# Up-projections with 512-column matmuls and a later add; modulation sums 20 to 23 on GpSimd

## The chip, the cores and the metric

The kernel runs on one core of a Trainium2 chip. The metric is the device time of one execution in microseconds (us), the median of several runs. Engines are TensorE (PE; PEld is its weight load), VectorE (DVE), ScalarE (ACT), GpSimd (POOL) and SyncE (SP), which here only issues the DMAs of the weights.

## The reference

Two transformer layers on 256 tokens with width 2048, in float32. The part that matters here is the end of the first layer:

```python
sh1, sc1, g1, sh2, sc2, g2 = split(silu(c) @ w_ada + b_ada, 6)      # w_ada: 2048 x 12288
h2 = modulate(rms_norm(x_new, norm2_w), sh2, sc2)                    # 256 x 2048
u = h2 @ w_up                                                        # w_up: 2048 x 11264
u = sum(pad(u)[:, j:j + T] * conv_w[j] for j in range(3)) + conv_b   # along the tokens
gate, val = split(u, 2)                                              # 5632 columns each
x_new = x_new + g2 * ((silu(gate) * val) @ w_down)                   # w_down: 5632 x 2048
```

`g2` is the last sixth of the modulation vector: parts 20 to 23 of it in the kernel, 512 numbers each.

## The kernel before

**Weights as a stream.** All weights pass through TensorE once, as one stream of chunks of 512 KB (`Stream`), in an order that is written out: two row blocks of 128 rows (k) by 512 columns. SP walks the stream (L519): for each chunk it waits until the chunk that last had the same place in SBUF is released, then issues the DMA. The waits are in program order, so one place that is late holds back every later chunk. A place is the least recently used one. There are four places, and up to job `uv1` three more; from then on each chunk takes the place of the chunk four before it in the stream.

**High and low parts.** To keep float32 accuracy on the fast matmul path, ACT rounds a chunk into a high part (`round_chunk`, L1324) and DVE subtracts to get the low part (`rest_chunk`, L1921); that subtraction releases the place. There are three pairs of such parts, so the rounding of chunk s waits for the matmuls of chunk s-3. ACT and DVE both work two chunks ahead of PE in program order. Products are hi\*act_hi, hi\*act_lo and lo\*act_hi (`three`), accumulated in PSUM by `gemm_chunk` (L648).

**Up-projections.** `w_up` has 22 jobs of 8 chunks, `ug0`, `uv0`, ..., `ug10`, `uv10` (gate and value, four tiles of 128 features each). Six pairs (96 chunks) run, then the first part of the down-projection (`downa`), then five pairs (80 chunks) and `downb`. A chunk is 2 k x 4 tiles x 3 products = 24 matmuls of 256 columns (all tokens). Two tiles share a PSUM bank: gate jobs use banks 0 and 1, value jobs 2 and 3. Sixteen steps of `hidden_units` run beside a pair: ACT scales the middle tap out of PSUM (`centre`, L1689), DVE adds the outer taps (`taps`, L2350, L2352), then the gate (L2370, L2373) and the split into `fR` (L1939, L1941).

**Modulation parts 20 to 23.** Each has eight chunks of `w_ada`, which stand in the stream beside the first six pairs: `beside(..., 5, 2, 14)` puts two of them among every five chunks of `w_up`, alternately after three and after two. With two DVE instructions of 512 columns per chunk, `sum_chunk` multiplies each of the chunk's two row blocks by a number per partition and adds it to `rows[a % 2]` (L1970, L1973), in DVE's program order right after a `rest_chunk`. That releases the chunk's place (semaphore `modulation_summed`). After the eighth, PE adds over the partitions into bank 5 (`ada_fold`, L745) and DVE adds the result to `g2b` (`spread_keep`, L1991). POOL issues a few DMAs in this part of the kernel and computes nothing.

Of the kernel before, what the change touches and what calls it, by code (L numbers as in the profile page):

```python
# [11 lines left out]
ACT = mybir.ActivationFunctionType  # L12
# [48 lines left out]
def shape_constants():  # L61
# [11 lines left out]
    def rotation(half):  # L73
# [48 lines left out]
       ("qn0", 2112, 384), ("qn1", 2496, 384), ("ks", 3200, 192), ("kvw", 3392, 460)]  # L122
O2_PAIRS = [6, 7, 4, 5, 0, 1, 2, 3]
# [16 lines left out]
for _names in (["gq", "gr0", "gr1", "dq0", "dq1"] + [f"{k}{n}" for k, c in (("gate", 8), ("pg", 4), ("pd", 4), ("out", 4))  # L140
                                                      for n in range(c)],
               [f"u{'gv'[v]}{i}" for i in range(KF // 4) for v in range(2)],
               [f"downa{n}" for n in range(4)], [f"downb{n}" for n in range(4)],
               ["km", "vm"] + [n for n, _, _ in IN2] + [f"{k}{n}" for k in ("uq", "ukv") for n in range(4)]
               + [n for n, _, _ in ZJOBS],
               [f"o2{n}" for n in range(4)]):
# [17 lines left out]
class Stream:  # L164
# [4 lines left out]
    def __init__(self):  # L169
# [23 lines left out]
        self.beside(ups[:KFA // 2], ada, range(20, 24), 5, 2, 14)  # L193
# [57 lines left out]
    def beside(self, jobs, ada, parts, num, den, first=0):  # L251

        todo = [(a, i) for a in parts for i in range(len(ada[a]))]
        at = {}
# [12 lines left out]
    def before(self, name):  # L269


        tiles, turns = 0, [0] * 4
        for job in self.job:
            if self.kind[self.job[job][0]]:
                continue
            for b in BANKS[job]:
                turns[b] += 1
            if job == name:
                return tiles, turns
            tiles += len(BANKS[job]) - 1  # L280

# [31 lines left out]
def build(nc, dram, out_dram, x_spill):  # L313
    st = Stream()
    ctx = ExitStack()
    with ctx:
# [211 lines left out]
        def _(pool):  # L528
# [47 lines left out]

            pool.wait_ge(S("diff_pv_done"), 8)
# [9 lines left out]
            pool.dma_start(g2b, dram["b_ada"][0:1, 5 * D:6 * D].to_broadcast([P, D])).then_inc(S("spread_bias"), 16)  # L587
            pool.wait_ge(S("mem_ready"), 8)
# [29 lines left out]
        def _(pe):  # L618
            mm = nc.tensor.matmul
            turns = [0] * 4  # L620
# [6 lines left out]
            def gemm_chunk(job, q, products):  # L627


                g = st.job[job][q]  # L630
                first, final = q == 0, q == len(st.job[job]) - 1
                pe.wait_ge(S("weights_split"), st.nth[g] + 1)
                w, row, kt, kp, col, width = st.chunks[g]
                k0 = sum(st.chunks[x][2] for x in st.job[job][:q])
                hi, lo = half(g, 0), half(g, 1)
                todo = [products(k0 + k, hi[:, k, :], lo[:, k, :]) for k in range(kt)]
                tiles = len(todo[0])
                opened = set()
                for m in range(tiles):
                    key = todo[0][m][0]  # L640
                    b = key // 2
                    if first and turns[b] and key not in opened:
                        pe.wait_ge(S(f"bank_emptied{b}"), turns[b])
                    for k in range(kt):
                        _, out, pairs = todo[k][m]
                        for n, (lhsT, rhs) in enumerate(pairs):
                            end = final and k == kt - 1 and n == len(pairs) - 1
                            last = mm(out, lhsT, rhs, start=first and key not in opened, stop=end,  # L648
                                      skip_group_check=True)
# [33 lines left out]
            def features(s, act, width=512, m=P):  # L683

                def products(k, hi, lo):
                    a = [act[0][:, k, :], act[1][:, k, :]]
                    return [(4 * s + 2 * (n // 2), bank(2 * s + n // 2, n % 2 * T, T)[0:min(m, width - c), :],
                             three(a, hi[:, c:min(c + m, width)], lo[:, c:min(c + m, width)]))
                            for n, c in enumerate(range(0, width, m))]
                return products  # L690
# [32 lines left out]
            def ada_fold(a):  # L723
# [481 lines left out]
            def second_block():  # L1205
                for step in range(ATT + 60):
# [5 lines left out]
                    if step == 10:  # L1212
                        pe.wait_ge(S("cmp_blocks_ready"), 1)
# [8 lines left out]
                    if step == 43:  # L1222
                        pe.wait_ge(S("cmp_rows_copied"), 2)
                        pe.wait_ge(S("low_ready"), 2)
                        for m in range(2):
                            mm(bank(4, 16 * m, NCMP)[0:96, :], hrow[:, 96 * m:96 * m + 96], hsel, start=True, stop=True)
                        mm(bank(5, 0, NCMP), hrow[:, 192:320], hsel, start=True, stop=True).then_inc(S("cmp_folded"), 1)
                    if step == 48:
                        pe.wait_ge(S("cmp_hidden"), 1)
                        for m, n in ((0, P), (1, 64)):  # L1230
# [4 lines left out]
                           ).then_inc(S("cmp_projected"), 1)  # L1235
                    a = step - ATT
                    if a == 0:
                        pe.wait_ge(S("cmp_done"), 1)
# [79 lines left out]
        def _(act):  # L1318
# [363 lines left out]
            def centre(s, i, b):  # L1682
# [3 lines left out]
                src, emptied = filled(f"u{'gv'[s]}{i}", b)  # L1686
                for m in (2 * b, 2 * b + 1):
                    f = KF * s + 4 * i + m
                    last = A(ftap[s][:, m, :], src[:, m % 2 * T:(m % 2 + 1) * T], ACT.Identity, bias=V("conv_b", f),  # L1689
# [3 lines left out]
            def hidden_units(first, last):  # L1693

                for n in range(16 * (last - first) + 6):
                    i, r = first + n // 16, n % 16
                    if r in (8, 9):
                        centre(0, i, r - 8)
# [3 lines left out]
                    if i > first and r in (0, 1):  # L1702
                        centre(1, i - 1, r)
# [89 lines left out]
            def second_block():  # L1793
                for step in range(ATT + 60):
# [6 lines left out]
                    if step == 46:  # L1801
                        act.wait_ge(S("cmp_bounded"), 1)
# [97 lines left out]
        def _(dve):  # L1900
# [437 lines left out]

            def taps(s, i, b):

                dve.wait_ge(S("taps_centred"), 4 * i + 2 * s + b + 1)
                src = bank(2 * s + b)
                for tap in (0, 2):
                    for m in (2 * b, 2 * b + 1):
                        f = KF * s + 4 * i + m
                        w = V("conv_w", 2 * KF * tap + f)
                        u = src[:, m % 2 * T:m % 2 * T + T]
                        y = ftap[s][:, m, :]
                        if tap == 0:
                            last = stt(y[:, 1:T], u[:, 0:T - 1], w, y[:, 1:T], ALU.mult, ALU.add)  # L2350
                        else:
                            last = stt(y[:, 0:T - 1], u[:, 1:T], w, y[:, 0:T - 1], ALU.mult, ALU.add)  # L2352
                    if tap == 0:
                        dve.drain()
                last.then_inc(S(f"bank_emptied{2 * s + b}"), 1)
# [4 lines left out]
            def hidden_units(first, last):  # L2360

                for n in range(16 * (last - first) + 6):
                    i, r = first + n // 16, n % 16
                    if r in (9, 10):
                        taps(0, i, r - 9)
                    if i > first and r in (1, 2):
                        taps(1, i - 1, r - 1)
# [93 lines left out]
            def blocks():  # L2461
# [19 lines left out]
                last.then_inc(S("cmp_blocks_ready"), 1)  # L2481
# [62 lines left out]
            def second_block():  # L2544
                for step in range(ATT + 60):
# [17 lines left out]
                    if step == 45:  # L2563
                        dve.wait_ge(S("cmp_folded"), 1)
                        ts(two(hexp[0:96, 0:32]), two(hk), -87.0, None, ALU.max)
                        ts(hexp[:, 32:32 + NCMP], hv, -87.0, None, ALU.max).then_inc(S("cmp_bounded"), 1)
                    if step == 47:
# [3 lines left out]
                        tt(hidv[:, 0:NCMP], hexp[:, 32:32 + NCMP], hv, ALU.mult).then_inc(S("cmp_hidden"), 1)  # L2571
                    if step == 50:
                        dve.wait_ge(S("cmp_projected"), 1)
# [3 lines left out]
                        v.tensor_copy(vcmp[0:NCMP, :], bank(7, 0, P)[0:NCMP, :]).then_inc(S("cmp_done"), 1)  # L2577
# [113 lines left out]
```

## Time and profile before

| | us |
|---|---|
| median of 3 runs (2324.26 to 2325.66) | 2325.04 |
| the profiled execution | 2324.98 |
| its span | 2323.2 |
| PE busy | 2240.4 (96%) |
| DVE busy | 1485.7 (64%) |
| ACT busy | 1038.5 (45%) |
| POOL busy | 47.3 (2%) |

The span is what the trace covers; about 1.8 us of the execution lie around it. Busy is time in which an engine ran an instruction; "idle before" in a row is how long the engine had waited, and the name behind the arrow is what ended that wait.

### The profile page before, as it was taken

To read this page: it belongs to the slowest core of one execution; us is meant where nothing else is said; L and a number is where in the kernel's file an instruction comes from. 1 tells how busy PE (TensorE), PEld (TensorE's weight loads), DVE (VectorE), ACT (ScalarE), POOL (GpSimd) and SP (SyncE) were. 2 spreads that over 40 slices of the span, in tenths; PEclk is the share of its full clock that TensorE was granted. 3 is DMA by queue.
4 is the path that set the end of the run, shared out by engine and by line. 5 is a ranking of instruction groups with operands and counts; after the bars stand their busy time and mean duration, and the time that the engine had idled before them with its cause. 6 is when DMAs were issued, how large, how long until landed. Compare 5 with 4: busy or idle time off the path is not lost.

```text
span 2323.2 us, 37359 instructions
## 1 busy us (share of the span) xinstructions
PE 2240.4 (96%) x15465; PEld 2010.0 (87%) x15465; DVE 1485.7 (64%) x2116; ACT 1038.5 (45%) x1429; POOL 47.3 (2%) x61
## 2 busy tenths in 40 slices
PE   5899999999999999989999999999999999999997
PEld 2577777899888999779999988999978898999986
DVE  3346766387476478777888855566665644576664
ACT  3134343354555643344444433444454534454444
POOL 3000000021000000000000000000000000000000
PEclk9899999999999999999999999999999999999999
DMA  9956766454444578866778655555545566544454
GB/s 364 369 163 197 230 210 197 145 151 146 127 137 129 187 243 280 293 230 206 227 243 260 225 190 190 183 185 183 185 165 196 166 189 201 170 128 137 129 198 145
DMA packets 249738, 458.75 MB, mean 197 GB/s; under 512 B 18995, under 2 KB 43889, under 8 KB 248160
## 3 DMA queue, kind: packets, MB, share of 16 engines
q1 hardware_dynamic: 246496, 442.47, 58.7%
q0 software_dynamic: 2496, 9.69, 1.1%
q10 hardware_dynamic: 576, 4.19, 0.5%
q8 instruction: 122, 2.00, 0.3%
q14 instruction: 48, 0.39, 0.0%
HBM read 454.20 MB, written 2.10 MB: 196 GB/s over the span
## 4 chain that ended last, share of the span: by engine, by line
PE 82%; DVE 7%; ACT 3%; DMA 3%; DVEq 2%; issue 2%; SPq 1%; ACTq 0%
PE psum L648 73%; DVE fast L1921 2%; PE psum L625 2%; DVE sbuf L1973 2%; ACT fast L1324 1%; DMA sbuf<-in_w_ada 1%; PE psum L1157 1%; DVEq L1972 1%; PE psum L904 1%; PE psum L959 1%; PE psum L719 1%; DVE fast L1941 1%; DMA sbuf<-in_w_up 1%; PE psum L978 1%; PE psum L1187 1%
## 5 line engine op out<-in xcount | busy, mean ns | idle before, releaser
L648 PE MATMUL psum<-fast,fast 128*128 128x256 f32 (+1 forms) x13424 | 2034.2, 312 | 20.6 <-DVE fast L1921 14.4
L648 PEld LDWEIGHTS psum<-fast,fast 128*128 128x128 f32 x13424 | 1848.6, 191 | 195.4 <-issue 46.6
L1921 DVE TENSOR_TENSOR fast<-sbuf,fast 128x1024 fp32r<-128x1024 f32 (+5 forms) x685 | 784.0, 1152 | 678.5 <-ACT fast L1324 671.2
L1324 ACT ACTIVATE fast<-sbuf 128x1024 fp32r<-128x1024 f32 (+4 forms) x689 | 682.1, 998 | 1046.0 <-PE psum L648 911.5
L1973 DVE SCALAR_TENSOR_TENSOR sbuf<-sbuf,sbuf 128x512 f32<-128x512 f32 x210 | 157.8, 751 | 18.3 <-issue 0.5
L1324 ACT ACTIVATE sbuf<-psum 128x512 f32<-128x512 f32 (+4 forms) x193 | 85.6, 469 | 79.9 <-PE psum L648 33.3
L625 PE MATMUL psum<-sbuf,sbuf 128*128 128x128 f32 (+2 forms) x349 | 58.7, 284 | 22.3 <-DMA sbuf<-in_consts 10.5
L625 PEld LDWEIGHTS psum<-sbuf,sbuf 128*128 128x128 f32 (+2 forms) x349 | 42.7, 145 | 33.0 <-DMA sbuf<-in_consts 10.5
L1941 DVE TENSOR_TENSOR fast<-sbuf,fast 128x512 fp32r<-128x512 f32 (+1 forms) x61 | 53.4, 876 | 4.5
L1689 ACT ACTIVATE sbuf<-psum,sbuf 128x256 f32<-128x256 f32 x88 | 44.2, 552 | 0.0
L2352 DVE SCALAR_TENSOR_TENSOR sbuf<-psum,sbuf,sbuf 128x255 f32<-128x255 f32 x88 | 38.5, 478 | 3.6 <-issue 0.4
L1514 ACT ACTIVATE sbuf<-psum,sbuf 128x512 f32<-128x512 f32 x32 | 22.0, 689 | 39.1 <-DVE sbuf L2171 38.3
L2350 DVE SCALAR_TENSOR_TENSOR sbuf<-psum,sbuf,sbuf 128x255 f32<-128x255 f32 x88 | 38.2, 475 | 0.0
L1939 DVE CAST fast<-sbuf 128x512 fp32r<-128x512 f32 (+1 forms) x61 | 31.5, 516 | 5.2 <-ACT sbuf L1390 1.6
L719 PE MATMUL psum<-sbuf,sbuf 128*32 128x256 f32 x312 | 24.9, 430 | 7.1 <-DMA sbuf<-in_w_ada 6.9
L572 POOL TENSOR_TENSOR sbuf<-sbuf,sbuf 128x1024 f32<-128x1024 f32 x8 | 19.3, 2412 | 508.1 <-ACT sbuf L1324 451.3
L719 PE MATMUL psum<-sbuf 128*32 128x256 f32 x200 | 15.8, 424 | 14.2 <-DMA sbuf<-in_w_ada 14.2
L1157 PE MATMUL psum<-sbuf 128*128 128x256 f32 (+1 forms) x112 | 25.6, 333 | 0.0
L1953 DVE TENSOR_TENSOR sbuf<-psum,sbuf 128x8 f32<-128x8 f32 x8 | 1.3, 164 | 36.4 <-PE psum L735 36.4
L1973 DVE SCALAR_TENSOR_TENSOR sbuf<-sbuf,sbuf,sbuf 128x512 f32<-128x512 f32 x30 | 22.5, 751 | 2.5
L719 PEld LDWEIGHTS psum<-sbuf,sbuf 128*32 128x32 f32 x312 | 8.0, 114 | 18.6 <-DMA sbuf<-in_w_ada 14.4
L719 PEld LDWEIGHTS psum<-sbuf 128*32 128x32 f32 x200 | 5.5, 114 | 20.9 <-DMA sbuf<-in_w_ada 10.7
(263 smaller groups left out, 962.6 us busy)
## 6 DMA issues: line engine op xcount, KB each, us to landing
sbuf<-in_w_ada SPq DMA_DIRECT2D x192, 512.0 KB, 4.9
sbuf<-in_w_up SPq DMA_DIRECT2D x176, 512.0 KB, 4.4
sbuf<-in_w_in SPq DMA_DIRECT2D x154, 512.0 KB, 3.8
sbuf<-in_w_down SPq DMA_DIRECT2D x88, 512.0 KB, 4.3
sbuf<-in_w_gate SPq DMA_DIRECT2D x64, 512.0 KB, 3.6
sbuf<-in_w_out SPq DMA_DIRECT2D x64, 512.0 KB, 4.8
sbuf<-in_w_proj_gla SPq DMA_DIRECT2D x16, 512.0 KB, 4.7
sbuf<-in_w_proj_diff SPq DMA_DIRECT2D x16, 512.0 KB, 5.9
```

Source lines behind the costliest of these rows:

```text
L625: return nc.tensor.transpose(out, in_, C("ident", n)[:, 0:n])
L648: last = mm(out, lhsT, rhs, start=first and key not in opened, stop=end, skip_group_check=True)
L719: last = mm(bank(ROWS_BANK[a], 0, T)[r, :], csil[:, k, :], w[:, j, T * h:T * h + T], start=k < 2, stop=k >= 14, skip_group_check=True)
L1157: last = mm(out, lhsT, rhs, start=k == 0, stop=k == len(terms) - 1)
L1324: return A(out, in_, ACT.Copy, scale=scale)
L1689: last = A(ftap[s][:, m, :], src[:, m % 2 * T:(m % 2 + 1) * T], ACT.Identity, bias=V("conv_b", f), scale=V("conv_w", 2 * KF + f))
L1921: last = tt(lo, raw, hi.bitcast(F32), ALU.subtract)
L1939: v.tensor_copy(hi, x)
L1941: return tt(lo, x, hi.bitcast(F32), ALU.subtract)
L1973: last = stt(sums, w[:, j, :], csil[:, k, 0:1], sums, ALU.mult, ALU.add)
L2350: last = stt(y[:, 1:T], u[:, 0:T - 1], w, y[:, 1:T], ALU.mult, ALU.add)
L2352: last = stt(y[:, 0:T - 1], u[:, 1:T], w, y[:, 0:T - 1], ALU.mult, ALU.add)
```

## The change

Two edits, cut to what matters; the rest of the diff renames semaphores of another part of the kernel and joins them.

The products of a chunk (PE). One matmul takes the high weights against both halves of the activations, 512 columns into a whole bank; a second takes the low weights against the high half, 256 columns. Gate jobs now use banks 0 to 3 and value jobs 4 to 7.

```diff
+for _i in range(KF // 4):
+    BANKS[f"ug{_i}"], BANKS[f"uv{_i}"] = (0, 1, 2, 3), (4, 5, 6, 7)
...
+            def wide(first, act):
+                def products(k, hi, lo):
+                    return [(2 * b, cut(bank(b), 2, T),
+                             [(hi[:, m * P:(m + 1) * P], act[:, :, k, :]),
+                              (lo[:, m * P:(m + 1) * P], act[:, 0, k, :], bank(b, 0, T))])
+                            for m, b in enumerate(range(first, first + 4))]
...
-                    gemm(f"u{'gv'[v]}{i}", features(v, hL), norm2_chunk if (i, v) == (0, 0) else None)
+                    if (i, v) == (0, 1):
+                        pe.wait_ge(S("units_read"), 8)
+                    gemm(f"u{'gv'[v]}{i}", wide(4 * v, XR[:, 0, :, :, :]), norm2_chunk if (i, v) == (0, 0) else None)
```

The add of the two halves: ACT copies the second half of two banks to `ftap`, DVE adds it to the first half in PSUM; `centre` and `taps` then read the first half and run one step later.

```diff
+            def copy_halves(s, i):
...
+                for b in range(2):
+                    filled(f"u{'gv'[s]}{i}", 2 * b)
+                    filled(f"u{'gv'[s]}{i}", 2 * b + 1)
+                    copy(ftap[s][:, 2 * b:2 * b + 2, :], cut(banks(4 * s + 2 * b), 2, 2, T)[:, :, 1, :]
+                         ).then_inc(S("halves_copied"), 1)
...
+            def halves(s, i):
+                for b in range(2):
+                    dve.wait_ge(S("halves_copied"), 4 * i + 2 * s + b + 1)
+                    pair = cut(banks(4 * s + 2 * b), 2, 2, T)
+                    tt(pair[:, :, 0, :], pair[:, :, 0, :], ftap[s][:, 2 * b:2 * b + 2, :], ALU.add).then_inc(S("halves_added"), 1)
```

The sums of parts 20 to 23 (POOL). The order of the stream and the places stay as they are.

```diff
+            def sum_chunks(a, first, final):
+                sums = rows[a % 2]
+                for i in range(first, final):
+                    g = st.job[f"ada{a}"][i]
+                    if i == 0:
+                        pool.wait_ge(S("ada_folded"), a - 1)
...
+                    pool.wait_ge(S(st.landed(g)[0]), st.landed(g)[1])
+                    w = ring(g)
+                    nc.gpsimd.tensor_tensor(w, w, csil[:, 2 * i:2 * i + 2, 0:1].to_broadcast([P, 2, 512]), ALU.mult)
+                    pool.drain()
+                    if i == 0:
+                        last = nc.gpsimd.tensor_tensor(sums, w[:, 0, :], w[:, 1, :], ALU.add)
+                    else:
+                        nc.gpsimd.tensor_tensor(sums, sums, w[:, 0, :], ALU.add)
+                        pool.drain()
+                        last = nc.gpsimd.tensor_tensor(sums, sums, w[:, 1, :], ALU.add)
+                    last.then_inc(S("modulation_summed"), 1)
...
+            for a in range(20, 24):
+                sum_chunks(a, 0, 8)
...
                 for a, i in st.sums_at.get(s, ()):
-                    sum_chunk(a, i)
+                    if a < SPREAD:
+                        sum_chunk(a, i)
```

The fold uses bank 5, now a bank of the value jobs, so it moves to a step in which that bank is free, and both sides wait for each other:

```diff
-                    self.fold_at[s + 2] = self.keep_at[s + 3] = a
+                    f = s + (4 if a >= SPREAD else 2)
+                    while quiet and (f - base) % 16 not in quiet:
+                        f += 1
+                    self.fold_at[f] = self.keep_at[f + 1] = a
...
+                        if b == 5 and 20 in st.folded_before(st.nth[g]):
+                            pe.wait_ge(S("g2_kept"), len(st.folded_before(st.nth[g])))
...
+                    if turns[5]:
+                        pe.wait_ge(S("value_banks_emptied"), 4 * (turns[5] - 1) + 2)
```

## Rows read from the trace of the kernel before

**Rows 1.** The page: busy time of each engine (us, share, instructions).
```profile
PE 2240.4 (96%) x15465; PEld 2010.0 (87%) x15465; DVE 1485.7 (64%) x2116; ACT 1038.5 (45%) x1429; POOL 47.3 (2%) x61
```

**Rows 2.** Stretches, L648 on PE alone: from:to, length, PE busy (matmuls), clock, DMA share, GB/s.
```profile
1500.00:1650.00 150.00, 150.00 (x1253) 1.00 0.58 183
1340.00:1430.00 90.00, 90.00 (x391) 1.00 0.56 189
```

**Rows 3.** Timeline of SP, 1130 to 1306 us: start, length, DMAs issued.
```profile
1130.34 0.37 SPq L519 DMA_DIRECT2D sbuf<-in_w_ada  x1
...
1204.90 0.37 SPq L519 DMA_DIRECT2D sbuf<-in_w_ada  x1
...
1219.44 0.37 SPq L519 DMA_DIRECT2D sbuf<-in_w_ada  x1
...
1302.25 3.42 SPq L519 DMA_DIRECT2D sbuf<-in_w_up  x2
```

**Rows 4.** Timeline of DVE there: start, length, instruction, [idle before <- what ended it].
```profile
1128.73 1.58 DVE L1973 SCALAR_TENSOR_TENSOR sbuf<-sbuf,sbuf 128x512 f32<-128x512 f32 x2
...
1203.30 1.57 DVE L1973 SCALAR_TENSOR_TENSOR sbuf<-sbuf,sbuf 128x512 f32<-128x512 f32 x2 [0.45 <-DMA sbuf<-in_w_ada]
...
1217.83 1.58 DVE L1973 SCALAR_TENSOR_TENSOR sbuf<-sbuf,sbuf 128x512 f32<-128x512 f32 x2
...
1300.65 1.58 DVE L1973 SCALAR_TENSOR_TENSOR sbuf<-sbuf,sbuf 128x512 f32<-128x512 f32 x2
```

**Rows 5.** Timeline of PE: start, length, matmuls.
```profile
1134.70 1.02 PE L745 MATMUL psum<-sbuf,sbuf 128*128 128x512 f32 x2
...
1311.40 1.02 PE L745 MATMUL psum<-sbuf,sbuf 128*128 128x512 f32 x2
1311.85 28.51 PE L648 MATMUL psum<-fast,fast 128*128 128x256 f32 x144
```

**Rows 6.** `w_ada` tiles, 1150 to 1320 us: from issue to landing.
```profile
DMA to landing us min/median/max: 3.5/4.4/5.2
```

**Rows 7.** Waits, 1150 to 1320 us: who for whom, us in total, times, longest.
```profile
ACT fast L1324 <- DMA sbuf<-in_w_up: 51.1, 28, 3.7
```

**Rows 8.** Timeline of POOL: start, length, instruction.
```profile
0.74 0.53 POOL L542 MEMSET sbuf<- 128x512 f32 x1 [0.29 <-POOLq L2676]
...
14.34 0.97 POOL L558 MEMSET sbuf<- 128x1024 f32 x1
15.60 0.49 POOL L561 DMA_DIRECT2D sbuf<-in_w_a_up_f  x1 [0.29 <-POOL sbuf L558]
...
470.75 2.40 POOL L572 TENSOR_TENSOR sbuf<-sbuf,sbuf 128x1024 f32<-128x1024 f32 x1 [451.31 <-ACT sbuf L1324]
...
546.78 2.88 POOL L575 TENSOR_TENSOR sbuf<-sbuf 128x1024 f32<-128x1024 f32 x1
```

**Rows 9.** Timeline of DVE beside two of those instructions.
```profile
471.84 2.40 DVE L1921 TENSOR_TENSOR fast<-sbuf,fast 128x1024 fp32r<-128x1024 f32 x1 [3.01 <-ACT fast L1324]
...
546.67 1.23 DVE L1921 TENSOR_TENSOR fast<-sbuf,fast 128x1024 fp32r<-128x1024 f32 x1 [0.47 <-ACT fast L1324]
547.83 2.91 DVE L2195 TENSOR_TENSOR sbuf<-sbuf,sbuf 128x1024 f32<-128x1024 f32 x1
```

**Rows 10.** Groups, 1135 to 1311 us: instructions, busy and mean ns, idle before.
```profile
L1921 DVE TENSOR_TENSOR fast<-sbuf,fast 128x1024 fp32r<-128x1024 f32 x59 | 71.6, 1222 | 19.7 <-ACT fast L1324 17.8
L1324 ACT ACTIVATE fast<-sbuf 128x1024 fp32r<-128x1024 f32 x60 | 63.7, 1061 | 96.9 <-DMA sbuf<-in_w_up 51.1 <-PE psum L648 45.8
L1973 DVE SCALAR_TENSOR_TENSOR sbuf<-sbuf,sbuf 128x512 f32<-128x512 f32 x45 | 33.8, 751 | 4.1 <-DMA sbuf<-in_w_ada 0.5
L745 PE MATMUL psum<-sbuf,sbuf 128*128 128x512 f32 x6 | 3.1, 590 | 0.0
```

**Rows 11.** Groups of the whole span, PSUM operands of 512 columns.
```profile
L1324 ACT ACTIVATE sbuf<-psum 128x512 f32<-128x512 f32 x96 | 54.7, 595 | 41.9 <-PE psum L648 29.1 <-PE psum L625 11.6 <-PE psum L904 1.1
L1991 DVE TENSOR_TENSOR sbuf<-sbuf,psum 128x512 f32<-128x512 f32 x8 | 5.4, 680 | 0.0
```

**Rows 12.** Stretch 1550 to 1600 us: busy of PE, PEld, DVE, ACT, POOL, clock, DMA.
```profile
1550.00:1600.00 50.00, 50.00 (x419) 50.00 (x418) 34.05 (x44) 23.00 (x27) 0.00 (x0) 1.00 0.57 184
```

More of the change, by code:

```diff
@@ L122 @@
        ("qn0", 2112, 384), ("qn1", 2496, 384), ("ks", 3200, 192), ("kvw", 3392, 460)]
+COMPRESSION_MULTIPLIED = {"folded": 1, "projected": 2}
+COMPRESSION_VALUES = {"blocks_ready": 1, "bounded": 2, "hidden": 3, "done": 4}
+SPREAD = 20
 O2_PAIRS = [6, 7, 4, 5, 0, 1, 2, 3]
@@ L192, in __init__ @@
         ups = [(f"u{'gv'[v]}{i}", panel("w_up", DFF * v + 512 * i, 512)) for i in range(KF // 4) for v in range(2)]
-        self.beside(ups[:KFA // 2], ada, range(20, 24), 5, 2, 14)
+        self.beside(ups[:KFA // 2], ada, range(20, 24), 5, 2, 14, (4, 5, 6))
         c = KFA * P
@@ L249, in add, with beside @@
             self.counts[kind] += 1
-    def beside(self, jobs, ada, parts, num, den, first=0):
+    def beside(self, jobs, ada, parts, num, den, first=0, quiet=None):
         todo = [(a, i) for a in parts for i in range(len(ada[a]))]
-        at = {}
+        at, base = {}, self.counts[0]
         for n, x in enumerate(todo):
@@ L280, in before, with folded_before @@
             tiles += len(BANKS[job]) - 1
+    def folded_before(self, s):
+        return [a for step, a in self.fold_at.items() if a >= 20 and step < s]
     def landed(self, g):
@@ L619, in _ @@
             mm = nc.tensor.matmul
-            turns = [0] * 4
+            turns = [0] * 8
             side = iter(())
@@ L642, in gemm_chunk @@
                     if first and turns[b] and key not in opened:
-                        pe.wait_ge(S(f"bank_emptied{b}"), turns[b])
+                        if b == 5 and 20 in st.folded_before(st.nth[g]):
+                            pe.wait_ge(S("g2_kept"), len(st.folded_before(st.nth[g])))
+                        if b < 4:
+                            pe.wait_ge(S(f"bank_emptied{b}"), turns[b])
+                        else:
+                            pe.wait_ge(S("value_banks_emptied"), 4 * (turns[b] - 1) + b - 3)
                     for k in range(kt):
                         _, out, pairs = todo[k][m]
-                        for n, (lhsT, rhs) in enumerate(pairs):
+                        for n, (lhsT, rhs, *part) in enumerate(pairs):
                             end = final and k == kt - 1 and n == len(pairs) - 1
-                            last = mm(out, lhsT, rhs, start=first and key not in opened, stop=end,
+                            last = mm(part[0] if part else out, lhsT, rhs, start=first and key not in opened, stop=end,
                                       skip_group_check=True)
@@ L1226, in second_block @@
                             mm(bank(4, 16 * m, NCMP)[0:96, :], hrow[:, 96 * m:96 * m + 96], hsel, start=True, stop=True)
-                        mm(bank(5, 0, NCMP), hrow[:, 192:320], hsel, start=True, stop=True).then_inc(S("cmp_folded"), 1)
+                        mm(bank(5, 0, NCMP), hrow[:, 192:320], hsel, start=True, stop=True).then_inc(S("compression_multiplied"), 1)
                     if step == 48:
-                        pe.wait_ge(S("cmp_hidden"), 1)
+                        pe.wait_ge(S("compression_values"), COMPRESSION_VALUES["hidden"])
                         for m, n in ((0, P), (1, 64)):
@@ L1701, in hidden_units @@
                         A(fsig, ftap[0], ACT.Tanh, scale=0.5).then_inc(S("ffn_tanh"), 1)
-                    if i > first and r in (0, 1):
-                        centre(1, i - 1, r)
+                    if i > first and r == 0:
+                        copy_halves(1, i - 1)
+                    if i > first and r in (1, 2):
+                        centre(1, i - 1, r - 1)
                     yield
@@ L2363, in hidden_units @@
                     i, r = first + n // 16, n % 16
[L2364 to L2367, printed above, removed]
+                    if r == 8:
+                        halves(0, i)
+                    if r in (10, 11):
+                        taps(0, i, r - 10)
+                    if i > first and r == 0:
+                        halves(1, i - 1)
+                    if i > first and r in (2, 3):
+                        taps(1, i - 1, r - 2)
                     if i > first and r == 3:
@@ L2480, in blocks @@
                                   ALU.add)
-                last.then_inc(S("cmp_blocks_ready"), 1)
+                last.then_inc(S("compression_values"), 1)
             def two(flat):
```

45 lines of the change are left out of this document (24 added, 21 removed).

## The prediction

> **What bounds the kernel now.** I read the engines' busy times first: PE is busy 96% of the span [rows 1], so what shortens its work shortens the kernel, as long as the weights arrive. Then the stretches of L648: in the second set of up-projections PE never idles at full clock, and starts a 256-column matmul every 150/1253 = 0.1197 us; in the down-projection, 512 columns every 90/391 = 0.2302 us [rows 2]. The third view is where PE's supply is thin: beside the first set of up-projections, ACT waits 28 times, 51.1 us in all, for chunks of `w_up` [rows 7]. The reader is to see who holds the places there. In the timelines of SP and DVE, the `w_ada` DMAs at 1130.34, 1204.90 and 1219.44 start 0.03 us after a sum of DVE ends (1128.73 + 1.58, 1203.30 + 1.57, 1217.83 + 1.58) [rows 3, 4]. That is the rule "four before": every second chunk of `w_ada` takes the place of the `w_ada` chunk ahead of it. From the first such pair (part 21's first chunk behind part 20's last) to part 23's seventh chunk there are 12 such links, and the seventh up chunk of `uv5`, issued at 1302.25 when the sum of 1300.65 ends [rows 3, 4], takes the last one's place.
>
> **Matmuls of 512 columns.** A chunk streams 24 x 256 = 6144 columns before, 8 x 512 + 8 x 256 = 6144 after; eight instructions fewer. A down-projection chunk streams the same 6144 in 12 instructions. So 24 x 0.1197 = 2.873 us against 12 x 0.2302 = 2.762: 0.111 us for 12 instructions, 9.2 ns each. Eight fewer save 0.074 us per chunk (pitch 2.799), over 176 chunks 13.0 us. Bounds: nothing, if half of the work with 256 columns keeps today's rhythm, and 0.111 x 176 = 19.5 us.
>
> **The added copy and add.** Per job ACT copies two times 512 columns, 0.595 us each, and DVE adds two times, 0.680 us each [rows 11]. Over 22 jobs that is 26 us of ACT and 30 us of DVE. In the second set DVE is busy 34.05 and ACT 23.00 of 50 us [rows 12]; the adds bring 1.36 us per 22 us. Both lie beside PE; the work on banks of a job has some five chunks (14 us) before the banks are wanted again. Cost 0; without that cover at most one pair's 1.3 us per job. Nothing of what was renamed costs time.
>
> **Sums leave DVE.** The 45 instructions of 0.751 us in rows 10 go (64 in all). DVE was not idle enough to keep up there: with them it ran late, and its sums had to be done in its order. What is late next is the sum itself on POOL.
>
> **Sums on POOL: the duration P of one chunk.** POOL takes 2.40 us for 1024 columns with two inputs in SBUF [rows 8]. Its 512-column instruction isn't in the trace; its memsets take 0.53 against 0.97 [rows 8], a ratio of 0.55, so 1.32 us (bounds: half, 1.20, and all, 2.40). Product and two sums: 2.40 + 2 x 1.32 = 5.04. Two drains: between 0 and the 0.29 us that POOL needs after a memset that it waits for [rows 8]; I take 0.1 each: 5.24.
> To this comes what POOL and DVE cost each other. The DVE subtraction at 471.84 takes 2.40 us in place of 1.22: POOL's instruction began at 470.75 and ended at 473.15, and the subtraction ends 1.09 later [rows 8, 9]. So with a two-input instruction in its way DVE waits for POOL's to end. The other way round, POOL's instruction at 546.78 starts beside a subtraction that ends at 547.90 and takes 2.88, 0.47 more [rows 8, 9]. A pair of links holds six POOL instructions, some 12 us, in which DVE has about five such instructions (one subtraction per chunk and L2370, L2373, L1941, L1939 once in 16). I let four of them get in between: 4 x 0.47 / 2 = 0.94 per chunk, P = 6.2. Bounds: 4.8 (halves of 2.40, no drain, nothing in the way) and 5.24 + 6 x 1.09 / 2 + 0.4 = 8.9.
> The Trainium skill, SBUF — State Buffer, section "Who interferes with whom", says that a VectorE instruction with two SBUF inputs and a GpSimd instruction that reads SBUF exclude each other for the whole instruction. The trace agrees for DVE (1.18 us lost at 471.84) and shows less on POOL's side (0.47); by the rule at full price on both sides P would be 5.24 + 4 x 1.09 / 2 = 7.4, and the sum below 28 us more.
>
> **What P does.** Before, a sum was done when DVE came to it, and the DMA behind it was hidden by chunks in stock. Now the pair is a chain: DMA of the even chunk, which can't start before the odd one is summed, then its sum, then the sum of the odd one, which has landed meanwhile: L + 2P per five chunks of `w_up`. L is 4.4 us (3.5 to 5.2) [rows 6]. 4.4 + 12.4 = 16.8 us, where PE needs 5 x 2.80 = 14.0. SP waits in order, so the chunks of `w_up` behind wait too, and PE starves.
> The stretch from 1130.34 (part 21's first chunk issued) to 1311.85 (PE starts `uv5`'s seventh chunk) [rows 3, 5] lasts 181.5 us before. After: 11 links of L + 2P, the last even chunk L + P, the up chunk L, its rounding 1.06 and subtraction 1.22 [rows 10], hand-offs some 0.6: 13 L + 23 P + 2.9 = 57.2 + 142.6 + 2.9 = 202.7 us. That is 21.2 more. If PE set the pace it would be 60 x 2.80 = 168.0, and 4.4 from 1130.34 to the fold behind chunk 33 (1134.70), and two folds of 0.45 (1311.40 to 1311.85) [rows 5]: 173.3.
> Before the stretch, six or seven places give POOL 14 us for two chunks of 6.2: nothing is late. The release at 1130.34 comes at the same place among the chunks, within 1 us. Outside the stretch 116 chunks save 0.074 each: 8.6 us. DVE's delays behind POOL's instructions (about 1.1 us a time) lie in time in which PE waits for DMAs anyway, and DVE works two chunks ahead (some 3 us of cover); without it 1 us at the end of the chain.
>
> **Folds.** They stay four, 0.59 us matmuls [rows 10]. The new wait is PE's for the value banks: `taps` of step 3 end about 1 us before the fold in step 4, and behind it only the next chunk is queued. 0, at most 1 us each. The consts DMA of POOL stands behind the sums and is wanted 400 us later.
>
> **The sum.** 2324.98 - 8.6 + 21.2 = 2337.6 for the profiled execution, whose time is that of the median (2325.04): 2338 us. The chain alone turns the sign: break-even is 23 P = 181.5 + 8.6 - 60.1, P = 5.65.
>
> **Rivals.**
> (a) POOL keeps up. P stays under 4.9 (its 512-column instructions near 1.2 us, DVE seldom in the way, and L shorter since fewer DMAs run at once). Then PE sets the pace: 173.3 - 181.5 - 8.6 = -16.8, 2308. With P = 5.24 and L = 4.0: 175.4, -14.7, 2310. For it: the 1024-column row is short, and the queue is empty when an even chunk is issued. Against: 2.40 us plus two sums is already 4.8.
> (b) Between: P = 5.65, the chain costs what the matmuls save: 2325.
> (c) The lock decides. Each DVE instruction holds POOL for its whole 1.09 us, five to a pair: P = 8.0, 13 L + 23 P + 2.9 = 244, 2379. It decides from P = 7 on, where 2P fills PE's 14 us alone. For it: rows 9 show full blocking one way; against: 0.47 the other way.
> (d) The 512-column matmuls don't do what they say: no saving outside the stretch, chain as forecast: 2346.
> The slower cases are all one mechanism, the even chunk's place.
>
> **How the numbers follow.** This kernel's changes can be told from about 0.2%, 4.7 us. Forecast (P from 5.9 to 7, 2330 to 2356): 0.52. (a) 0.25. (b), within 4.7 us of before, 0.12. (c) 0.06. (d) 0.05, slower too. Slower 0.63, same 0.12, faster 0.25. Range: from (a) at 2310 to P = 7.2 at 2361; the forecast's own is 2330 to 2356.
>
> **What would show it.** In the changed kernel's trace: POOL busy for about 32 x 6 us in 96 instructions, 1.3 to 1.8 us for those of 512 columns; the even `w_ada` DMAs issued as a POOL instruction ends, 16 to 17 us apart; PE idle in that stretch alone, a few us per link, released by L1921 behind a DMA; subtractions of 1.22 us stretched to over 2; in the second set 16 matmuls per 2.80 us. I am wrong if the even issues are 14 us apart, or if PE waits for banks or for DVE outside the stretch.

## The result

The changed kernel takes 2356.34 us, median of 4 runs (2354.22 to 2364.18); the kernel before, beside it, 2325.35. The ratio is 1.0143, 95% interval 1.0131 to 1.0156: 33 us slower by the ratio, 31 by the medians, 32 by the two profiled executions. The forecast was 13 us slower, 2338. The sign and the chain of the forecast were there; the size was less than half, because a second cause was costed at nothing.

The profiled execution took 2356.95 us, its span is 2355.1. First the line of the page that answers to [rows 1], then two stretches of PE's matmuls (L686, before L648): one of the second set of up-projections, one of the first.

```profile
PE 2241.4 (95%) x14057; PEld 1937.9 (82%) x14057; DVE 1519.9 (65%) x2096; ACT 1059.2 (45%) x1473; POOL 225.4 (10%) x153
```
```profile
1500.00:1650.00 150.00, 150.00 (x851) 130.14 (x851) 1.00 0.59 186
```
```profile
1100.00:1300.00 200.00, 176.08 (x959) 148.55 (x958) 153.01 (x148) 86.60 (x108) 126.31 (x66) 0.98 0.63 209
```

The first stretch shows L686 on PE and PEld alone, in the second set, without idle time: 16 matmuls per 150/851 x 16 = 2.820 us, where 24 took 2.873. The other shows all engines in the first set (PE, PEld, DVE, ACT, POOL): PE does 959/16 = 60 chunks in 200 us and idles 24, DVE is busy 153, POOL 126.

To see where the time went, take the first DMA of `w_up` and the first DMA of the job behind the down-projection (`w_mem_kv`) as borders. Below, "the section" is the time between the two. The lines give the times at which the first and the last DMA of each tensor were issued.

```profile
L529 SPq DMA_DIRECT2D sbuf<-in_w_up x176: 367/368/1107, 1006.1 to 1694.0; - x176
L529 SPq DMA_DIRECT2D sbuf<-in_w_mem_kv x16: 367/368/368, 1818.5 to 1865.2; - x16
```
In the kernel before the same lines:
```profile
L519 SPq DMA_DIRECT2D sbuf<-in_w_up x176: 367/368/368, 1008.5 to 1664.0; - x176
L519 SPq DMA_DIRECT2D sbuf<-in_w_mem_kv x16: 367/368/368, 1787.4 to 1834.1; - x16
```

The section between them grew from 778.9 to 812.4 us, by 33.5; ahead of it 2.4 went, in work that is the same in both, and behind it came 0.8. Each part of the section is counted from its own first DMA to the first DMA of the next: first set 299.9 before, 335.5 after (+35.6), `downa` 128.7 and 129.4, second set 229.9 and 226.1 (-3.8), `downb` 120.4 and 121.3. Nearly the whole loss lies in the first set, where the sums of parts 20 to 23 run.

Timelines of the changed kernel in one link of the chain, SP, then DVE, then POOL (the lines that answer to [rows 3, 4, 8]). A link runs from one even `w_ada` chunk to the next; even is the chunk that takes the place of another `w_ada` chunk, odd the one behind it, which takes the place of a chunk of `w_up`.

```profile
1253.02 0.37 SPq L529 DMA_DIRECT2D sbuf<-in_w_ada  x1
1254.10 6.30 SPq L529 DMA_DIRECT2D sbuf<-in_w_up  x2
1264.49 0.37 SPq L529 DMA_DIRECT2D sbuf<-in_w_ada  x1
1264.91 4.91 SPq L529 DMA_DIRECT2D sbuf<-in_w_up  x3
1275.91 0.37 SPq L529 DMA_DIRECT2D sbuf<-in_w_ada  x1
```
```profile
1257.09 2.92 DVE L1984 TENSOR_TENSOR fast<-sbuf,fast 128x1024 fp32r<-128x1024 f32 x1
1260.10 2.14 DVE L2447 TENSOR_TENSOR sbuf<-sbuf 128x1024 f32<-128x1024 f32 x1
1262.17 2.30 DVE L1984 TENSOR_TENSOR fast<-sbuf,fast 128x1024 fp32r<-128x1024 f32 x1
```
```profile
1251.71 1.29 POOL L605 TENSOR_TENSOR sbuf<-sbuf,sbuf 128x512 f32<-128x512 f32 x1
1256.70 2.23 POOL L598 TENSOR_TENSOR sbuf<-sbuf 128x1024 f32<-128x1024 f32 x1 [3.71 <-DMA sbuf<-in_w_ada]
1259.07 2.09 POOL L603 TENSOR_TENSOR sbuf<-sbuf,sbuf 128x512 f32<-128x512 f32 x1
1261.31 2.08 POOL L605 TENSOR_TENSOR sbuf<-sbuf,sbuf 128x512 f32<-128x512 f32 x1
1268.83 2.35 POOL L598 TENSOR_TENSOR sbuf<-sbuf 128x1024 f32<-128x1024 f32 x1 [5.45 <-DMA sbuf<-in_w_ada]
```

The even chunk is issued at 1253.02, 0.02 us after POOL's last sum ends: the chain as forecast. It is summed by 1263.39. The odd chunk should have been in SBUF by then. It is issued only at 1264.49, as DVE's subtraction ends (1262.17 + 2.30). The subtraction at 1257.09, the product L2447 and this subtraction took 2.92, 2.14 and 2.30 us where 1.22 is usual, each beside a POOL instruction: 1.7, 0.9 and 1.1 us lost. POOL then idles 5.45 us. This link takes 22.9 us. Over the eleven links from 1131.84 to 1326.04 the mean is 17.65, about 15.5 where the odd chunk is there in time, up to 23 where it isn't, and POOL's idle time ahead of odd chunks sums to 21.0.

Groups of the changed kernel: from 1000 to 1700 us POOL's instructions and DVE's rounding copy, then from 1130 to 1300 us DVE's subtraction (before, 1222 ns [rows 10]):

```profile
L598 POOL TENSOR_TENSOR sbuf<-sbuf 128x1024 f32<-128x1024 f32 x29 | 62.4, 2153 | 84.0 <-DMA sbuf<-in_w_ada 84.0
L605 POOL TENSOR_TENSOR sbuf<-sbuf,sbuf 128x512 f32<-128x512 f32 x28 | 52.0, 1857 | 4.0
L603 POOL TENSOR_TENSOR sbuf<-sbuf,sbuf 128x512 f32<-128x512 f32 x28 | 50.3, 1797 | 4.3 <-issue 0.4
L2002 DVE CAST fast<-sbuf 128x1024 fp32r<-128x1024 f32 x10 | 10.7, 1070 | 0.9
```
```profile
L1984 DVE TENSOR_TENSOR fast<-sbuf,fast 128x1024 fp32r<-128x1024 f32 x50 | 81.7, 1647 | 40.2 <-ACT fast L1375 39.5
```

### The profile page after: what moved, and what is told of

Read it like the earlier page. It is cut to its first block, busy times and chain, and to the rows that moved or that the text cites. A ratio compares the mean times of both kernels' runs of the same rounds, so it can differ in the third digit from the quotient of the medians.

```text
span 2355.1 us, 34692 instructions
## 1 busy us (share of the span) xinstructions
PE 2241.4 (95%) x14057; PEld 1937.9 (82%) x14057; DVE 1519.9 (65%) x2096; ACT 1059.2 (45%) x1473; POOL 225.4 (10%) x153
## 4 chain that ended last, share of the span: by engine, by line
PE 76%; DVE 7%; issue 4%; DMA 3%; POOLq 3%; ACT 3%; DVEq 2%; POOL 2%; SPq 1%; ACTq 0%
PE psum L686 67%; DVE fast L1984 2%; PE psum L658 2%; POOLq L599 2%; DMA sbuf<-in_w_ada 2%; ACT fast L1375 1%; POOL sbuf L605 1%; POOLq L604 1%; DVE sbuf L2036 1%; PE psum L1208 1%; PE psum L766 1%; PE psum L953 1%; PE psum L1008 1%; DVE fast L2004 1%; DMA sbuf<-in_w_in 1%
## 5 line engine op out<-in xcount | busy, mean ns | idle before, releaser
L686 PE MATMUL psum<-fast,fast 128*128 128x512 f32 (+2 forms) x12016 | 2031.4, 329 | 54.3 <-DVE fast L1984 48.5
L686 PEld LDWEIGHTS psum<-fast,fast 128*128 128x128 f32 (+1 forms) x12016 | 1774.3, 190 | 300.2 <-DVE fast L1984 57.3
L1984 DVE TENSOR_TENSOR fast<-sbuf,fast 128x1024 fp32r<-128x1024 f32 (+5 forms) x685 | 826.8, 1216 | 681.8 <-ACT fast L1375 677.0
L1375 ACT ACTIVATE sbuf<-psum 128x512 f32<-128x512 f32 (+4 forms) x237 | 108.9, 490 | 78.0 <-PE psum L686 32.9
L2036 DVE SCALAR_TENSOR_TENSOR sbuf<-sbuf,sbuf 128x512 f32<-128x512 f32 x155 | 116.5, 751 | 13.4 <-issue 0.5
L598 POOL TENSOR_TENSOR sbuf<-sbuf 128x1024 f32<-128x1024 f32 x29 | 62.4, 2153 | 84.0 <-DMA sbuf<-in_w_ada 84.0
L605 POOL TENSOR_TENSOR sbuf<-sbuf,sbuf 128x512 f32<-128x512 f32 x28 | 52.0, 1857 | 4.0
L603 POOL TENSOR_TENSOR sbuf<-sbuf,sbuf 128x512 f32<-128x512 f32 x28 | 50.3, 1797 | 4.3 <-issue 0.4
```

The costliest lines, as they stand in the source:

```text
L598: nc.gpsimd.tensor_tensor(w, w, csil[:, 2 * i:2 * i + 2, 0:1].to_broadcast([P, 2, 512]), ALU.mult)
L603: nc.gpsimd.tensor_tensor(sums, sums, w[:, 0, :], ALU.add)
L605: last = nc.gpsimd.tensor_tensor(sums, sums, w[:, 1, :], ALU.add)
L686: last = mm(part[0] if part else out, lhsT, rhs, start=first and key not in opened, stop=end, skip_group_check=True)
L1375: return A(out, in_, ACT.Copy, scale=scale)
L1984: last = tt(lo, raw, hi.bitcast(F32), ALU.subtract)
```

## The experiments

"Section" is the time defined above, in the one profiled execution of each kernel; it leaves out what varies from run to run ahead of it and behind it (1544 to 1553 us over these kernels). Time is the median, ratio is to the kernel before, run beside it. "Places" is the number of places in SBUF during the up-projections. Where there are five, the first DMA of the next part leaves one chunk earlier, and some 2.8 us pass from the first set to the second (e6: 294.8 and 232.7, before: 299.9 and 229.9): first sets are compared only between kernels with the same number of places, and sections otherwise.

| kernel | sums on | places | section us | time us | ratio (95%) |
|---|---|---|---|---|---|
| before | DVE | 4 | 778.9 | 2325 | 1 |
| changed | POOL | 4 | 812.4 | 2356.3 | 1.0143 (1.0131, 1.0156) |
| e1 matmuls alone | DVE | 4 | 780.3 | 2327.5 | 1.0011 (1.0002, 1.0021) |
| e2 sums' move alone | POOL | 4 | 812.2 | 2357.0 | 1.0139 (1.0124, 1.0154) |
| e3 changed, fifth place | POOL | 5 | 795.4 | 2342.0 | 1.007 (1.0054, 1.0087) |
| e4 POOL writes only | none | 4 | 785.1 | 2333.0 | 1.0034 (1.0025, 1.0043) |
| e7 e4, fifth place | none | 5 | 764.7 | 2313.1 | 0.9949 (0.9935, 0.9962) |
| e11 changed, one sum less | POOL | 4 | 788.7 | 2335.5 | 1.0048 (1.003, 1.0066) |
| e5 e1, fifth place | DVE | 5 | 775.6 | 2322.3 | 0.999 (0.9981, 0.9999) |
| e6 before, fifth place | DVE | 5 | 777.8 | 2324.9 | 1.0003 (0.9993, 1.0012) |
| e8 matmuls in set 2 alone | DVE | 5 | 775.3 | 2323.0 | 0.999 (0.9981, 0.9999) |
| e9 e5, spread thinner | DVE | 5 | 779.4 | 2326.6 | 1.001 (1.0001, 1.0019) |
| e10 e9, rounding on ACT | DVE | 5 | 767.1 | 2314.1 | 0.996 (0.9946, 0.9973) |
| e12 e5, rounding on ACT | DVE | 5 | 768.5 | 2314.9 | 0.9965 (0.9956, 0.9975) |

**e1, the matmuls alone.** The folds' earliest step is two behind the last chunk again, as in the kernel before; they are still moved on to a step in which bank 5 is free.
```diff
-            for a in range(20, 24):
-                sum_chunks(a, 0, 8)
...
-                    if a < SPREAD:
-                        sum_chunk(a, i)
+                    sum_chunk(a, i)
```


> Only the first edit: 512-column matmuls and the later add; the sums of parts 20 to 23 stay on DVE, the folds keep their new steps. Theory (the loss is the sums' move to POOL): 16 matmuls in 2.81 us instead of 24 in 2.86, outside the stretch of the sums 116 chunks x 0.06 = 7 us, in it little since DVE has the sums and the adds: 2314 to 2320. Rival (the new matmul form, the copies or the value banks cost time themselves): no faster than 2325.

2327.5: by its number the rival, not the theory. The second set gives its 3.8 us (226.1), the first set takes 2.9 more (302.8). DVE carries the sums and the new adds there and is busy 175.48 of 200 us (before, 167.94), so the new form costs there what it should have saved:
```profile
1100.00:1300.00 200.00, 191.59 (x1069) 163.38 (x1068) 175.48 (x222) 95.59 (x118) 0.00 (x0) 1.00 0.75 234
```

**e2, the sums' move alone.** The kernel before with POOL's `sum_chunks`.
```diff
+            for a in range(20, 24):
+                sum_chunks(a, 0, 8)
...
+                    if a < SPREAD:
+                        sum_chunk(a, i)
-                    self.fold_at[s + 2] = self.keep_at[s + 3] = a
+                    f = s + (4 if a >= SPREAD else 2)
+                    self.fold_at[f] = self.keep_at[f + 1] = a
```


> Only the second edit: sums of parts 20 to 23 on POOL, matmuls of 256 columns and banks 0 to 3 as before. Theory: the same even DMAs about 17.6 us apart, since neither L nor P knows the matmuls' form, so the stretch is about 213 us again, and without the matmuls' 7 us outside it the time is 2358 to 2366. Rival (the two edits hurt each other, by banks and folds): clearly under 2350.

2357.0, a microsecond under the range expected, the first set 332.9: the move alone makes the whole result, and the form of the matmuls hardly matters under it.

**e3, a fifth place.**
```diff
-         ("gate7", "uv1", [18080, 19104, 21152], ("diff_pv_done", 8))]
+         ("gate7", "uv1", [18080, 19104], ("diff_pv_done", 8)),
+         ("gate7", "downa3", [21152], ("diff_pv_done", 8))]
...
```


> The changed kernel with a fifth place for chunks from uv1 on to the end of downa (words that nothing else uses there), so that a chunk takes the place of the chunk five before it and no w_ada chunk stands behind another. Theory A (the place behind the odd chunk makes the chain): the chain is gone, PE sets the pace where DVE lets it: stretch 175 to 185 instead of 213, 2318 to 2330. Theory B (what costs is that DVE's subtractions wait for POOL's instructions): the contention is all there, 2345 or more.

**e4, POOL writes only.** The kernel leaves out the sums of parts 20 to 23; POOL holds each chunk for about as long by writing zeros.
```diff
-                    nc.gpsimd.tensor_tensor(w, w, csil[...].to_broadcast([P, 2, 512]), ALU.mult)
...
+                    for _ in range(5):
+                        nc.gpsimd.memset(w, 0.0)
+                        pool.drain()
+                    last = nc.gpsimd.memset(w[:, 0, 0:256], 0.0)
```


> The changed kernel with POOL's three instructions per chunk replaced by memsets of the chunk of about the same total (5 x 0.97 us, 0.3 us and drains, P about 5.8); the sums of parts 20 to 23 are left out. POOL then reads no SBUF, holds a w_ada chunk as long as before, and by theory doesn't hold up DVE. Theory A (chain alone): links stay as they are, 2350 or more. Theory B (DVE's waiting alone): 2318. Both together, that is, the chain L + 2P = 4.0 + 11.7 in each link, without the 21 us in which POOL waited for odd chunks and without the stalls ahead of the stretch: 2356 - 21 - 5 = 2330.

e3 took 2342.0 and e4 2333.0, so neither theory holds alone; the sum of both, 2330, came close for e4. Here and below, contention is that DVE's and POOL's instructions stretch one another. Without the chain 17 us of the section go (795.4), without the contention 27 (785.1). In e4 the even DMAs are still issued as POOL's last instruction ends, now 16.1 us apart on average: L of 4.0, twice a P of 5.8, and 0.5 of waiting for odd chunks, against 1.9 in the changed kernel. DVE's subtraction is back at 1223 ns (first line, e4), while in e3, where no chunk of `w_ada` takes the place of another, it reaches 1833 (second line):
```profile
L1982 DVE TENSOR_TENSOR fast<-sbuf,fast 128x1024 fp32r<-128x1024 f32 x54 | 65.9, 1223 | 54.6 <-ACT fast L1373 53.2
```
```profile
L1985 DVE TENSOR_TENSOR fast<-sbuf,fast 128x1024 fp32r<-128x1024 f32 x54 | 98.3, 1833 | 20.0 <-ACT fast L1376 18.9
```

**e7, both taken away.** The edits of e3 and e4 together; it too leaves out the sums of parts 20 to 23.

> Both causes taken away at once: the changed kernel with POOL's memsets in the place of its sums (it reads no SBUF; the sums of parts 20 to 23 are left out) and with the fifth place. With the chain alone the first set took 306.7 us, with the contention alone 315.8, with both 335.5. If these two are all that costs: 288 to 291 in the first set, PE-bound at 2.81 us a chunk, time 2309 to 2313. If something else in the change costs (folds, value banks, copies): above 294, over 2316.

2313.1, section 764.7, and PE without a gap at about 2.8 us per chunk:
```profile
1100.00:1300.00 200.00, 200.00 (x1146) 175.41 (x1146) 147.30 (x181) 105.55 (x130) 140.87 (x168) 1.00 0.80 258
```
With it the account closes to 3 us: from 764.7 the chain alone adds 20.4 (e4), the contention alone 30.7 (e3), both 47.6 (changed), where the plain sum is 51. These are single executions, e4's the fastest of its ten; by the medians the same account reads 19.9, 28.9 and 43.3. In the stretch above PE has no gap that anything else of the change could have caused.

**e11, a shorter sum.** The kernel leaves out POOL's second add of each chunk.
```diff
-                        pool.drain()
-                        last = nc.gpsimd.tensor_tensor(sums, sums, w[:, 1, :], ALU.add)
```


> The changed kernel with POOL's second 512-column add left out of each chunk (the sums lack every second row block), four places as in the changed kernel. POOL's time per chunk falls from 5.9 to about 3.9 us. Theory (two causes that add up, each in proportion): the chain L + 2P = 4.0 + 7.8 = 11.8 us is under PE's 14 and costs nothing; DVE waits for two POOL instructions in place of three, two thirds of the 31.8 us that contention alone cost: first set 284 + 21 = 305, time 2331 to 2336. Rival (contention costs only as part of the chain): first set under 295, under 2322.

2335.5 (two runs), as expected; the section is 24.0 over e7 where 21 was expected. With two reading instructions in place of three DVE's subtraction is at 1571 ns. P is 4.2 in the trace, so L + 2P is some 12 us, under PE's pace, and still about four fifths of the contention's cost stand (24.0 of 30.7). The loss doesn't need the chain.

**e5 and e6, the fifth place without POOL.** The edit of e3, in e1 and in the kernel before.

> The first edit alone (512-column matmuls, sums of parts 20 to 23 on DVE) with the fifth place. The first edit alone lost 2.9 us in the first set of up-projections (302.8 against 299.9) where its matmuls should have saved 5.5. Theory A (DVE, busy 44 of 50 us there with the sums and the new adds, sets the pace): the place changes little, the first set stays at 298 to 302, time 2322 to 2327. Theory B (the place of the w_ada chunks is what held it): the first set falls to 290 to 294, 2315.

> The kernel before with the fifth place alone. The first set took 299.9 us where 96 chunks of 2.87, the start and the folds make about 293 to 295. If the places held PE up in the kernel before too: first set 294 to 297, time 2319 to 2322. If it was DVE: 2325, no change.

2322.3 and 2324.9. The place gives e1 4.7 us in the section (775.6); DVE is busy 179.21 of 200 us, and the first set stays 10.6 above e7's: theory A by the time, with a part of B. The kernel before gains nothing that can be measured: there PE was at its pace but for 1 us.

**e8, 512 columns in the second set alone.** `up` takes `features` below pair 6 and `wide` from there on, and `centre`, `taps` and the banks follow.

> A version made from the findings: 512-column matmuls in the second set of up-projections alone (5 pairs, 80 chunks), where DVE has room; the first set and its sums on DVE as before, with the fifth place. Theory: the second set saves 3.8 us as in the changed kernel (229.9 to 226.1), the first set what the fifth place alone gives, 3 to 5: 2316 to 2319. If the second set's gain is lost again behind it (the changed kernel's downb was 0.9 longer): 2319 to 2321.

2323.0, 0.1% faster, short of what was expected: the section is 3.6 less than before, but the median only 1.7.

**e9, the chunks spread thinner.**
```diff
-        self.beside(ups[:KFA // 2], ada, range(20, 24), 5, 2, 14, (4, 5, 6))
+        self.beside(ups[:KFA // 2], ada, range(20, 24), 8, 3, 8, (4, 5, 6))
```


> A version made from the findings: 512-column matmuls in both sets, sums of parts 20 to 23 on DVE, the fifth place, and the 32 w_ada chunks spread thinner and from earlier on (8 chunks of w_up for 3 of w_ada, from the ninth, instead of 5 for 2 from the fifteenth). With the fifth place alone DVE was busy 179 of 200 us and the first set took 294.6 where 284.0 is PE's pace. Theory (DVE's load sets it): the sums take 0.375 in place of 0.4 of a chunk's 1.57 us, 0.04 us per chunk in which DVE is the bound: 1 to 3 us less, 2319 to 2321. Rival: the early chunks fall on DVE's busiest steps (second norm) and give it back: 2322 to 2325.

2326.6, slower than e5 and outside both ranges: the theory fails here. PE idles 8 of 200 us, released by DVE's subtraction. Why the thinner order is worse was not settled.

**e10 and e12, the rounding on ACT.**
```diff
-                        split_values(fR[0][...], fR[1][...], ftap[0]).then_inc(S("ffn_hidden"), 1)
+                        tt(fR[1][...], ftap[0], fR[0][...].bitcast(F32), ALU.subtract).then_inc(S("ffn_hidden"), 1)
...
+                    if i > first and r == 5:
+                        act.wait_ge(S("lambda_products"), 1 + i)
+                        copy(fR[0][...], ftap[0]).then_inc(S("lambda_exps"), 1)
```


> The same, and the rounding of the hidden values moves from DVE (0.69 us a pair) to ACT, which is busy half of the time; its subtraction on DVE runs one step later. Theory (DVE's load): another 0.5 us per pair of the first set, 2316 to 2320, and no change in the second set, which PE bounds. Rival (a wait between ACT and DVE costs more than 0.69 us): no faster than the version without it.

> The version with 512-column matmuls, sums on DVE, the fifth place and the rounding of the hidden values on ACT, with the w_ada chunks where they stand in the changed kernel (5 to 2, from the fifteenth). The thinner spread alone cost 3.7 us of the first set (298.3 against 294.6), and with the rounding on ACT the first set took 286.1, PE's pace being 284.0. Theory A (the spread costs by itself): 284 to 285 in the first set, 2311 to 2313. Theory B (once DVE has room the spread doesn't matter): 286, 2313 to 2315.

2314.1 and 2314.9: both faster than the kernel before by 0.35 to 0.40%, and within a microsecond of each other: with the rounding on ACT the order of the chunks matters by no more than that (1.4 us in the section). PE is at its pace again in the first set (e10):
```profile
1100.00:1300.00 200.00, 199.66 (x1138) 173.24 (x1136) 179.72 (x231) 107.55 (x134) 0.00 (x0) 1.00 0.79 252
```
The gain of 12 us in e10 against e9 is larger than the 0.69 us per pair that leave DVE. The copy, its drain and the subtraction stood in a row behind two others on DVE in the same steps; that this row of dependent instructions is what held PE is argued from the code, not shown.

## Why the prediction was too small

**The chain: right, and even a little too dear.** The even DMAs start as POOL's last sum ends. P was put at 6.2; the groups give 2.15 + 1.80 + 1.86 and two drains of 0.14, 6.1, and the spans in the eleven links 5.9. Its parts: the product takes 1.90 us undisturbed, not 2.40 (its second input is one number per partition, spread; that this is the reason was not tested), the sums 1.28 to 1.30 undisturbed (forecast 1.32) and 2.09 with DVE in the way (0.8 more, forecast 0.47). So the undisturbed P was put 0.5 too high (5.24 for 4.7) and the delays of POOL 0.3 too low (0.9 for 1.2): two errors that partly cancelled, which was luck. L was 3.7 to 4.6 in the eleven links, 4.0 on average, forecast 4.4. With 6.0 and 3.9 the forecast's own formula gives 13 x 3.9 + 23 x 6.0 + 2.9 = 191.6 us for the stretch, 11 less than forecast. Measured, from 1131.84 to PE's start of `uv5`'s seventh chunk at 1345.37: 213.5.
```profile
1345.37 14.94 PE L686 MATMUL psum<-fast,fast 128*128 128x512 f32 x71 [0.61 <-DVE fast L1984]
```

The size of this cost comes from contention as well. A chunk that DVE doesn't disturb takes 4.7 us on POOL:
```profile
1180.63 1.90 POOL L598 TENSOR_TENSOR sbuf<-sbuf 128x1024 f32<-128x1024 f32 x1
1182.67 1.27 POOL L603 TENSOR_TENSOR sbuf<-sbuf,sbuf 128x512 f32<-128x512 f32 x1
1184.08 1.27 POOL L605 TENSOR_TENSOR sbuf<-sbuf,sbuf 128x512 f32<-128x512 f32 x1
```
With that P a link would be 4.0 + 9.4 = 13.4 us, an estimate, under PE's 14: by this estimate the chain binds only because DVE stretches POOL's instructions. e4 kept the stretched P (5.8), so its 20.4 us are the chain at that P, and both causes would go back to the one contention. A kernel with memsets of 4.7 us per chunk, which would show it, was not run.

**The step that failed: DVE's delays were costed at nothing.** The prediction said that they "lie in time in which PE waits for DMAs anyway", and that the odd chunk "has landed meanwhile". The 21.0 us for which POOL waits ahead of odd chunks are about the 22 that the formula lacks. A place is released by DVE's subtraction; a subtraction that ends 1.1 us late behind a POOL instruction lets a DMA start 1.1 us late, and SP, in order, passes that on to the odd chunk, for which POOL waits, for which the next even chunk waits. PE's idle time was no cover, since DVE's delays make idle time of their own. e3 prices the contention alone at 30.7 us, without any chain. DVE is busy 174 of 200 us there, its waits for POOL included, and each of PE's idle times ends on DVE's subtraction. The rule of the Trainium skill that the prediction weighed (SBUF — State Buffer, "Who interferes with whom") was used for P alone; its other side, that DVE too is held up, is where most of the loss was. The same section says that a GpSimd instruction that only writes SBUF doesn't contend with a two-input VectorE instruction: e4 and e7 agree, 1223 and 1224 ns for the subtraction beside memsets.

**A term that the prediction didn't have: the clock.** PE idled up to 4 us at a time, and just behind the longest gaps its granted clock was lower. The first window below lies just behind the gap of 4.04 us that ended at 1325.66 (0.50, the lower level, 1.2 GHz, 10 matmuls in 3 us), the second begins 4 us behind the first (back at 1.00, 2.4 GHz, 25 in 4):
```profile
1326.00:1329.00 3.00, 3.00 (x10) 2.52 (x10) 3.00 (x4) 0.00 (x0) 0.00 (x0) 0.50 0.73 236
1333.00:1337.00 4.00, 4.00 (x25) 3.48 (x24) 4.00 (x2) 2.43 (x4) 3.71 (x3) 1.00 0.26 59
```
The six chunks from 1325.66 on took PE 19.10 us, where six at 2.80 are 16.8; five from 1186.66 on, behind 3.41 us of idling, took 15.73, where five took 14.14 from 1238.60 on. How much of the section this cost was not tested; it is part of what both causes are priced at above.

**Ahead of the stretch "nothing is late": wrong too.** From the first DMA of `w_up` to the first even chunk it took 1131.84 - 1006.1 = 125.7 us, against 1130.34 - 1008.5 = 121.8 before, where 2.4 less was forecast. PE idles there three times, 1.0 to 2.0 us, for DVE's subtraction, with six or seven places in use; in e4, without the contention, it doesn't. The prediction had named a wait of PE for DVE outside the stretch as a sign of being wrong.
```profile
1107.08 37.90 PE L686 MATMUL psum<-fast,fast 128*128 128x512 f32 x208 [1.96 <-DVE fast L1984]
```

The miss then adds up. The profiled execution was 32.0 us slower, 12.6 were forecast: the stretch gave 32.0 in place of 21.2, the part ahead of it 3.9 in place of -2.4, the second set -3.8 in place of -5.9.

**The matmuls.** The forecast was 9.2 ns per instruction and 0.074 us per chunk; the second set shows 2.873 - 2.820 = 0.053, and 3.8 us for 80 chunks where 5.9 was expected. The reason wasn't tested; that a part of the overhead isn't per instruction would fit. In the first set the saving was worth nothing at first: DVE got the adds (1.36 us per job, costed at 0) and, in e1, kept the sums. "Both lie beside PE" held in the second set, where DVE has room, and failed in the first. Where PE has no gaps, e7 against e6, the section is 13.1 us shorter, about the forecast's own 13.0, but divided otherwise, which is luck. In the first set, L649 of e6 and L685 of e7:
```profile
1100.00:1280.00 180.00, 179.12 (x1481) 177.85 (x1481) 1.00 0.79 248
1100.00:1280.00 180.00, 179.12 (x1025) 156.81 (x1025) 1.00 0.79 257
```
That is 2.90 us for 24 matmuls and 2.80 for 16, some 0.1 us per chunk, 10 us for 96 chunks, twice the rate of the second set. e7 has no sums on DVE either, so how much of this is the matmuls' form was not separated.

**Folds and banks.** Forecast 0, and e7, with the same folds and banks, has no idle time of PE between 1100 and 1300 us.

**Rivals.** (a) and (b) fell with the result. (c), the lock at full price on both sides, was put at 2379 by way of P; P stayed at 6, and the contention cost through DVE instead, a way that no rival had. (d), no saving by the matmuls, is half true, by DVE.

## What to carry to other kernels

Price a move from one engine to another by both engines' waits. If the trace shows their instructions stretched beside each other, as rows 8 and 9 did, the engine that was relieved is slowed by the one that took the work, and the other way round. In a ring whose places are released in order, a delay of the releasing engine isn't covered by idle time downstream, since that idle time is the delay. Take a suspected chain apart with a kernel that keeps its durations and drops the contention (memsets for sums), and one that keeps the contention and drops the dependence (one more place): two runs gave 20 and 31 us, and together with a third, without either, they closed the account to 3 us. The durations to keep are the undisturbed ones, or the dependence is priced with the contention in it.

## What the runs showed of the hardware

- POOL's `tensor_tensor` on 512 columns takes 1.28 us undisturbed and mostly 2.08 to 2.10 where DVE's two-input instruction is in the way; on 1024 columns 1.90 with a spread second input, 2.41 with a full one, 2.86 to 2.88 disturbed.
- DVE's 1024-column subtraction takes 1.22 us beside POOL's memsets (e4, e7). Beside POOL's sums the mean rises with the time that POOL is busy of 200 us: 1.57 at 99 (e11), 1.65 at 126 (changed), 1.70 at 132 (e2), 1.83 at 146 (e3).
- DVE's rounding copy (CAST) suffers as well: beside the sums five of them took 0.69, 0.69 (POOL idle), 1.61, 2.02 and 2.22 us. Unlike the subtraction it is also stretched beside memsets: 1.49 and 0.86 us in e7 with a memset running, 0.69 and 0.69 without.
- A `w_ada` DMA of 512 KB was in use 3.7 us after its issue at best.
- PE's granted clock was 0.50 just after it had idled 4.04 us, and 1.00 again in a window 7 us later.
